# Seven items of experts in place of eight, earlier condition rows and a fifteenth place for expert weights

## The reference

```python
def moe(h, w_router, b_router, w1, w3, w2):
    scores = jax.nn.softmax((h @ w_router).astype(jnp.float32), axis=-1)
    ...                                   # best group of 4 experts, two experts inside it
    gate = ...                            # (tokens, 16), two weights a token
    a = jnp.einsum('bld,edf->blef', h, w1)
    b = jnp.einsum('bld,edf->blef', h, w3)
    act = jax.nn.silu(a) * b * gate[..., None].astype(h.dtype)
    return jnp.einsum('blef,efd->bld', act, w2)

def trunk_layer(x, cond, p, layer, ...):
    mod = jax.nn.silu(cond) @ p['w_ada'] + p['b_ada']
    sh1, sc1, g1, sh2, sc2, g2 = jnp.split(mod, 6, axis=-1)
    h = rms_norm(x, p['norm1']) * (1 + sc1) + sh1
    ...                                   # attention, long convolution, retention
    x = x + g1 * (merged @ p['w_out'])
    h2 = rms_norm(x, p['norm2']) * (1 + sc2) + sh2
    x = x + g2 * moe(h2, ...)
```

## Time and profile before

| | |
|---|---|
| time, median of 3 | 1211.95 us (1210.23 to 1212.96) |
| profiled execution | 1209.46 us, span 1207.7 us |
| TensorE busy | 1144.6 us (95%) |
| VectorE, ScalarE busy | 510.8 us, 215.3 us |
| moved by DMA | 351.51 MB, mean 291 GB/s |
| chain that ended last | PE 83%, DMA 11%, DVE 3%, ACT 2% |
| mean granted clock | 0.978 |

### The profile page before, as it was taken

The page is one execution under the profiler, slowest core; times in us unless marked ns, Lnnn a source line. Parts: engine busy times, 40 slices in busy tenths (PEclk is TensorE's granted clock), DMA queues, the critical chain, the costliest instruction groups (busy, mean ns, idle before and its releaser), DMA issues.

```text
span 1207.7 us, 17513 instructions
## 1 busy us (share of the span) xinstructions
PE 1144.6 (95%) x6966; PEld 883.0 (73%) x6966; DVE 510.8 (42%) x1154; ACT 215.3 (18%) x452; POOL 41.2 (3%) x83
## 2 busy tenths in 40 slices
PE   6978999999999999989989999999999999998996
PEld 5667888878888775646548888888888877564653
DVE  2539877666736221111233876653252531111113
ACT  2240012232021100111124201223201210000011
POOL 1001110000000000000000111000000000000000
PEclk9998999999998999989999999999999899998999
DMA  9519874365459999999964578543434999999992
GB/s 384 219 70 347 310 283 172 142 261 223 183 205 423 421 421 386 422 420 421 420 261 161 180 279 276 188 161 132 139 140 177 418 421 420 371 422 420 421 420 101
DMA packets 55799, 351.51 MB, mean 291 GB/s; under 512 B 6960, under 2 KB 7136, under 8 KB 18336
## 3 DMA queue, kind: packets, MB, share of 16 engines
q1 hardware_dynamic: 51552, 337.75, 70.7%
q0 software_dynamic: 4160, 12.58, 2.8%
HBM read 346.08 MB, written 2.65 MB: 289 GB/s over the span
## 4 chain that ended last, share of the span: by engine, by line
PE 83%; DMA 11%; DVE 3%; ACT 2%; issue 1%; SPq 1%; DVEq 0%; ACTq 0%; POOLq 0%
PE bank L806 24%; PE bank L1102 12%; PE bank L1141 7%; PE bank L986 7%; PE bank L1007 5%; PE bank L801 5%; PE bank L1082 4%; PE bank L1182 4%; DMA lent<-in_experts 4%; DMA ring<-in_experts 4%; DMA ring<-in_weights 3%; PE bank L817 2%; PE bank L730 1%; PE bank L1117 1%; PE bank L1058 1%
## 5 line engine op out<-in xcount | busy, mean ns | idle before, releaser
L806 PE MATMUL bank<-h,ring 128*128 128x256 f32 x1472 | 327.4, 382 | 13.1 <-DMA ring<-in_weights 13.1
L806 PEld LDWEIGHTS bank<-h,ring 128*128 128x128 f32 x1472 | 279.0, 191 | 54.2 <-DMA ring<-in_weights 13.5
L1770 DVE SCALAR_TENSOR_TENSOR ring<-ring 128x1024 f32<-128x1024 f32 x128 | 151.7, 1223 | 17.5 <-DMA ring<-in_mod_weights 8.9
L1102 PE MATMUL bank<-lent,gates 128*64 128x256 f32 (+2 forms) x896 | 127.0, 380 | 2.3 <-ACT gates L1610 2.3
L1102 PE MATMUL bank<-ring,gates 128*64 128x256 f32 (+2 forms) x1024 | 121.0, 380 | 6.2 <-DMA ring<-in_experts 4.8
L1102 PEld LDWEIGHTS bank<-lent,gates 128*64 128x64 f32 (+2 forms) x896 | 82.6, 137 | 36.3 <-ACT gates L1610 2.8
L1102 PEld LDWEIGHTS bank<-ring,gates 128*64 128x64 f32 (+2 forms) x1024 | 80.0, 130 | 30.6 <-issue 6.8
L1141 PE MATMUL bank<-ring,gates 128*64 128x512 f32 (+2 forms) x304 | 83.7, 613 | 9.5 <-DMA lent<-in_experts 9.5
L1690 DVE SCALAR_TENSOR_TENSOR gates<-gates,bank 128x512 f32<-128x512 f32 (+1 forms) x16 | 10.5, 654 | 141.3 <-issue 108.9
L2262 DVE COPY uc<-bank 128x512 f32<-128x512 f32 x14 | 9.7, 692 | 132.4 <-PE bank L1141 132.4
L1141 PEld LDWEIGHTS bank<-ring,gates 128*64 128x64 f32 (+2 forms) x304 | 24.5, 135 | 54.2 <-issue 54.2
(11 more groups left out here) (268 smaller groups left out, 1141.8 us busy)
## 6 DMA issues: line engine op xcount, KB each, us to landing
ring<-in_experts SPq DMA_DIRECT2D x108, 1024.0 KB, 21.2
ring<-in_weights SPq DMA_DIRECT2D x96, 1024.0 KB, 6.5
lent<-in_experts SPq DMA_DIRECT2D x84, 1024.0 KB, 19.9
ring<-in_mod_weights SPq DMA_DIRECT2D x64, 512.0 KB, 5.6
lent<-lent POOLq DMA_DIRECT2D x48, 32.0 KB, 5.6
cst<-in_consts POOLq DMA_DIRECT2D x1, 1345.0 KB, 11.6
x<-in_x_in SPq DMA_DIRECT2D x1, 1024.0 KB, 5.0
ring<-in_cond_rows POOLq DMA_DIRECT2D x1, 1024.0 KB, 6.2
```

Source lines behind the costliest of these rows:

```text
L806: last = pe.matmul(bank[b][:, c * TOK:(c + 1) * TOK], w[:, k, c * P:(c + 1) * P], h[:, k, :], start=(k == 0), stop=(k == KT - 1))
L1102: last = pe.matmul(bank[b][rows, half * 256:half * 256 + 256], hgat[:, k, rows], w[j][:, k, :], start=(k == 0), stop=(k == KT - 1), skip_g ...
L1770: last = dve.scalar_tensor_tensor(out, w, 0.5, cond_wide[:, c, :], ALU.mult, ALU.mult, accum_out=mod_all[:, of, row, c:c + 1])
```

## The change

It does three things.

- Items: `pair`, `pair`, `triple`, `wide`, `triple`, `pair`, `triple`. A triple gives 64 columns to one expert and 32 to each of two. The last six of the sorted experts have rooms of 32 seats, not the last four. The item with a single expert and its own functions are gone, and the last item is a full one whose combine signals by bank.
- Condition rows: POOL fetches them when the pieces of `ada 1` are used, ScalarE takes the tanh behind unit 0, DVE multiplies behind unit 1. For this the opening's pieces use three places of `lent` in place of three of the ring.
- Places: the pieces of `ada 5` and the experts' may use every place of ring and lent once the merge has ended. The experts' may also use the memory of `h`, once `ada 5` is used. SP's waits for the stores and for the chunks stand ahead of these pieces.

```diff
-ITEM_KINDS = ("pair", "pair", "wide", "quad", "pair", "pair", "pair", "single")
+ITEM_KINDS = ("pair", "pair", "triple", "wide", "triple", "pair", "triple")
+WIDTHS = {"pair": (64, 64), "triple": (64, 32, 32), "wide": (128,)}
-ITEM_EXPERTS = ((12, 13), (14, 15), (0,), (8, 9, 10, 11), (1, 2), (3, 4), (5, 6), (7,))
+ITEM_EXPERTS = ((12, 13), (14, 15), (1, 6, 7), (0,), (2, 8, 9), (4, 5), (3, 10, 11))
+WIDE_ROOM, SMALL_ROOM, SMALL = 128, 32, 6
+TOKENS_SLOT = SLOTS + LENT
+OPENING_LENT = (SLOTS, SLOTS + 1, SLOTS + 2)
...
-    for (kind, layer, _), c in pieces:
-        lent = range(SLOTS, SLOTS + LENT) if kind == "moe" else ()
-        own = SLOTS if kind == "moe" or (kind, layer, _) in OPENING else LEAST
-        since = {at: free[at] for at in range(own)}
-        since.update({at: max(free[at], END["merge", layer, 5]) for at in lent})
+    for (kind, layer, number), c in pieces:
+        since = {at: free[at] for at in range(LEAST)}
+        if (kind, layer, number) in OPENING:
+            since.update({at: free[at] for at in OPENING_LENT})
+        elif kind == "moe" or (kind, number) == ("ada", 5):
+            since.update({at: max(free[at], END["merge", layer, 5]) for at in range(LEAST, SLOTS + LENT)})
+        if kind == "moe":
+            since[TOKENS_SLOT] = max(free[TOKENS_SLOT], END["ada", layer, 5])
...
+                if SLOT[n] in range(LEAST, SLOTS) and not given[layer]:
+                    sp.wait_ge(s_chunk_used, sum(CHUNKS[:layer + 1]))
+                    given[layer] = True
...
             for kind, layer, number in PLAN:
+                if (kind, number) == ("ada", 5):
+                    sp.wait_ge(s_stored, 16 * 4 * (layer + 1))
...
-                sp.wait_ge(s_stored, 16 * 4 * (layer + 1))
-                sp.wait_ge(s_chunk_used, sum(CHUNKS[:layer + 1]))
...
                     pool.wait_ge(s_weights_used, END["ada", 0, 1])
-                    pool.wait_ge(s_weights_used, MADE_FREE)
                     pool.dma_start(raw, cond_rows.broadcast_to([P, 2 * D])).then_inc(s_cond_moved, 16)
-                    pool.wait_ge(s_mod_ready, ada_at(0, 1) + 1)
+                    pool.wait_ge(s_weights_used, OPENING_END)
...
-                            for j in range(many):
-                                rows = slice(width * j, width * j + width)
+                            for j, rows in enumerate(ITEM_ROWS[p]):
                                 last = pe.matmul(bank[b][rows, half * 256:half * 256 + 256],
                                                  hgat[:, k, rows], w[j][:, k, :],
...
-                    if layer == 0 and u == 1:
+                    if layer == 0 and u == 0:
                         sc_e.wait_ge(s_cond_moved, 16)
...
-                    link(ts(extra, at, SORTED - 4.5, ALU.is_gt, float(SMALL_ROOM - BLOCK), ALU.mult))
+                    link(ts(extra, at, SORTED - SMALL - 0.5, ALU.is_gt, float(SMALL_ROOM - BLOCK), ALU.mult))
```

More of the change, by code:

```diff
@@ L49 @@
 ITEM_OUT = [2 * len(e) for e in ITEM_EXPERTS]
-ITEM_LAST = [2 if kind == "single" else len(e) for kind, e in zip(ITEM_KINDS, ITEM_EXPERTS)]
-WIDE_ROOM, SMALL_ROOM = 128, 32
-MORE = 2 * TOK // (BLOCK + 1)
+ITEM_ROWS = [[slice(sum(WIDTHS[kind][:j]), sum(WIDTHS[kind][:j + 1])) for j in range(len(WIDTHS[kind]))]
+             for kind in ITEM_KINDS]
+WIDE_ROOM, SMALL_ROOM, SMALL = 128, 32, 6
+MORE = 8
 OVER = (TOK - 1 - SMALL_ROOM) // BLOCK + 1
@@ L154, in ring_table @@
         used.append(since[at])
-        free[at] = gone[(kind, layer, _), c]
+        free[at] = gone[(kind, layer, number), c]
     return slot, count, used
@@ L198, in y_end @@
     if p == PAIRS:
-        return END["moe", layer, 0]
+        return END["moe", layer, 0] - ITEM_OUT[p] // 2 * (1 - half)
     return ff_end(layer, p + 1) + ITEM_OUT[p] // 2 * (half + 1)
@@ L613, in _ @@
                                                         max_val=SORTED - 1)
-                    for part in (0, 2, 1, 3) if ITEM_KINDS[p] == "single" else range(4):
+                    for part in range(4):
                         for j in range(many):
@@ L621, in _ @@
                 for part in (4, 5):
-                    fetch(expert(PAIRS, 0, part))
+                    for j in range(len(ITEM_EXPERTS[PAIRS])):
+                        fetch(expert(PAIRS, j, part))
             for c in range(4):
@@ L1106, in moe_in @@
                         last.then_inc(s_weights_used, many)
[L1108 to L1121, removed]
             def act_turn(layer, p):
@@ L1146, in moe_out, with combine @@
                         take(b)
-                last = combine(s_y_lo, ITEMS * layer + p + 1, s_y_hi, PAIRS * layer + p + 1,
-                               s_scat_ready, scat[p % 3], p == 0)
+                last = combine(s_y_lo, ITEMS * layer + p + 1, s_y_hi, ITEMS * layer + p + 1,
+                               s_scat_ready, scat[p % 3], p == 0, p == PAIRS)
                 last.then_inc(s_combined, 1)
[L1151 to L1175, removed]
+            def combine(lo, count, hi, hi_count, scat_event, matrix, fresh, by_bank=False):
                 pe.wait_ge(scat_event, count)
@@ L1185, in combine @@
                                      skip_group_check=True)
+                    if by_bank and dt % 2 and dt < KT - 1:
+                        last.then_inc(s_combined, 1)
                 return last
@@ L1284, in _ @@
                 gather(layer, 0)
-                for p in range(PAIRS):
+                for p in range(ITEMS):
                     moe_in(layer, p)
-                    gather(layer, p + 1)
+                    if p < PAIRS:
+                        gather(layer, p + 1)
                     act_turn(layer, p)
```

62 lines of the change are left out of this document (26 added, 36 removed).

## The result

The changed kernel takes 1319.57 us (1318.16 to 1321.24), 1.090 times the time of the kernel before (95% interval 1.0871 to 1.0925). The forecast was 1329, slower. The profiled execution took 1318.2 us with a span of 1316.4, 108.7 us more than before's 1207.7, where the prediction had 116.7.

A forecast was written before the change was run, and what follows sets the result against it. TensorE was taken to bound the dense stages and nearly tie with weight transfers in the expert stages. 2 x 66.1 - 15.5 = +116.7 on 1209.5 gives 1326.2, about 1329 on the median's scale; range 1160 to 1345.

The forecast's parts named there:

- What bounds the kernel: Whole kernel: dense stages are TensorE alone; expert stages a near-equal race of TensorE and weight transfers, DMA costing 10.4 us a layer.
- rival (a): Expert items: disjoint columns of different widths never wait, landings bound the stage, about 1171 us (1158 to 1185); chance 0.40.
- Early condition rows: Opening: fetching the rows earlier removes TensorE's 13.1 us wait near 83 us and the slow start after it, 15.5 us together.
- The fear that DVE: Opening: DVE gets only 10.9 us earlier, 4.6 less than TensorE, so later consumers may lose a little; bound 11 us.
- Places: Before the experts: pieces start at about 338 instead of 357, 19 us of head start, about 5 lost; price nothing.
- its cover: Expert stages: the places' worth depends on whether DMA still bounds; 45 us of weights hide under each triple.
- The count of pieces and places: Expert stage: 100 pieces of 2.49 us from 338, plus 5 us of full places, put the last landing at about 597.
- Seven items: Expert stages: one item removed saves 19.1 us; three mixed-width items add 31.9 each, 95.6, ending layer 0 at 686.1.
- the other side: Mixed items: disjoint column groups of different widths run side by side without waiting, so the kernel gets faster; chance 0.40.
- The sum: Whole kernel: two layers at 66.1 us more, less 15.5 in the opening, +116.7 us, about 1329.
- Removal of the single item: Expert stage, layer 0: dropping the one-expert item saves 19.1 us; without DMA waits the layer ends at 590.5.

The follow-up runs named there:

- with strips: Changed kernel, but a triple's 64-column expert runs as two 32-column matmuls with the same weights: 1170.99 us, ratio 0.967 to the kernel before.
- the kernel with one triple: Changed kernel, but only one triple in each layer (pair, pair, triple, wide, quad, pair, pair): 1211.61 us, ratio 1.0034 to the kernel before.

## Why the prediction was right

**What bounds the kernel.** Right. With TensorE's price of the triples gone, the stage is bound by landings and the time is 1171, the number that rival (a) gave, though the fall in the span was 36.4 us and not 41.5.

**Early condition rows.** Priced at 15.5, measured at 15.8 alone and 15.9 in the changed kernel (96.92 for 112.84). The fear that DVE, which is 12.3 us earlier with `z` (92.55 for 104.81), not 10.9, takes back a part didn't come true.

**Places.** Priced at nothing in the changed kernel, and its cover named: TensorE. The profile after has no wait of TensorE for an expert piece among its ten longest waits. The head start is in the DMA rates (406 for 231 GB/s). Where the cover is gone, the places are worth 11 to 13 us with strips. The count of pieces and places behind it gave 12, but it was at least 9 us short for the kernel with one triple. It moves pieces at a fixed rate and refills a place without delay; it isn't fine enough for single places.

**Seven items.** The step that decided. The trace of before showed changes of width only between columns that overlap, and the price was taken over to columns that don't. The prediction gave that 0.51 against 0.40 for the other side, so the sign was a choice between two near equals, made by an argument and not by a row. It held: 22.4 for an in product where the prediction had 22.7, 8.9 for an out product where it had 9.1, and a step of 1.13 us where it had 0.431 + 0.71 = 1.14. The rule of the Trainium skill, "TensorEngine Tiling (Array Packing)", Key Properties, that a change of the tiling mode drains TensorE, holds in this kernel for disjoint columns as well; the 0.134 us and the lost overlap are this case's numbers for it. The concurrency of column groups of the Trainium skill, "TensorE: Matmul & The Clock Gate", Part 3, holds for equal widths, four at a time, as the strips show.

**The sum.** 116.7 forecast, 108.7 measured in the span. Of the 8.0 us, 2.4 are in the two expert stages, which grew by 65.2 and 64.6 us and not by 66.1 each: a triple was 0.6 us cheaper, 3.6 for the six, and about a third of that was lost elsewhere in the stages. 0.4 are in the opening. Another 4.6 are the stretches between the output product and the first gather, 18.0 us in either layer before, 16.4 and 15.0 us in the changed kernel; no step of the prediction touched them, so that part of the error is not the mechanism's, and the last section is about them. The rest, 0.6, is spread over the dense stages and the end.

**Removal of the single item.** Forecast was an end at 590.5 without landings, so 208.7 us of stage in layer 0; 303.4 less three triples at 31.3 is 209.5.

## What to carry to other kernels

Give matmuls that are to share the array side by side one column width. Here 64 columns beside 32, in float32, cost 0.70 us a step more than one width did; other widths and types weren't tried. Fill a mixed item with strips of the smallest width and stream the wide one's data to several strips, which cost nothing here but instructions. Do not count on a slow item to hide the waits for transfers behind it: once the places are full the transfers slow down too, and in the kernel with one triple only a quarter to a third of its price came back. What more buffers are worth is read where the transfers bound the stage; the same rules for places were worth 4 us in one kernel and 11 to 13 in the other. An order of instructions can price a change between two kinds of work, but it shows a lost overlap only if the two kinds stand side by side in it.

## What the runs showed of the hardware that was not expected

The stretch between the output product and the experts took 18.0, 16.4 or 15.0 us with the same work on TensorE. Its rows (columns as above): the kernel before in layer 0, the changed one in layer 0 and in layer 1, and the one with strips in layer 0.

```profile
363.77:381.77 18.00, 17.25 (x153) 15.19 (x153) 10.21 (x47) 3.30 (x8) 0.53 (x1) 0.81 1.01 424
```

```profile
347.82:364.21 16.39, 15.64 (x154) 13.58 (x154) 10.21 (x47) 3.31 (x8) 0.53 (x1) 0.90 0.86 351
...
988.75:1003.78 15.03, 14.02 (x154) 11.96 (x154) 10.20 (x47) 3.30 (x8) 0.00 (x0) 1.00 0.84 338
```

```profile
348.25:366.25 18.00, 17.25 (x154) 15.19 (x153) 10.21 (x47) 3.31 (x8) 0.53 (x1) 0.81 0.78 314
```

The granted clock is 0.81, 0.90 and 1.00 of 2.4 GHz, a mean of the levels of 1.2 and 2.4 GHz in the first two. Beside the transfers it shows no order: the kernel before has 0.81 at 424 GB/s, the one with the early rows alone 0.90 at 423, the one with strips 0.81 at 314. The work ahead of the stretch doesn't tell them apart either: in the kernel before and in the changed one TensorE was busy without a gap for the 17.8 us ahead of it in layer 0, at a granted clock of 1.00. What decides is open. At 1.00 TensorE is no longer all of it: in layer 1 of the changed kernel the last 10.6 us of the stretch in the chain are VectorE's, save 0.2 of ScalarE. All this makes up to 3 us a layer that belong to no edit, as much as the fifteenth place is worth at most.
